# Decoder trunk, two layers, one core: six of twelve modulation sums move from TensorE to GpSimd

## The reference, cut to what matters

```python
def reference(x, c, ...):
    c_act = silu(c)
    for l in range(2):
        mod = c_act @ ada_w[l] + ada_b[l]              # 2048 -> 6144
        shift, scl, gate_res = split(mod, 3)
        h = _rms(x, norm_g[l]) * (1.0 + scl) + shift
        # layer 0: pooling mixer and block attention, layer 1: indexed attention and convolution
        y, g = branches_of(h @ w_in[l])
        x = x + gate_res * ((y * silu(g)) @ w_out[l])
    return x
```

## Time and profile before

| what | value |
|---|---|
| time, median of 3 runs | 983.06 us (979.67 to 984.81) |
| profiled execution, span | 977.3 us; its own time is not among those shown, median less span is 5.8 us |
| PE busy | 942.7 us (96%) |
| DVE busy | 822.4 us (84%) |
| ACT busy | 422.5 us (43%) |
| POOL busy | 63.5 us (6%), 76 instructions |
| granted TensorE clock, mean | 0.991 |

### The profile page before, as it was taken

One profiled execution on the slowest core, in us unless ns is written; L12 is line 12 of the kernel. 1 busy time (PEld: TensorE's weight loads), 2 busy tenths in 40 slices (PEclk: granted clock), 3 DMA queues, 4 the chain that ended last, 5 costly groups with the idle time before them and its releaser, 6 DMA issues.

```text
span 977.3 us, 18750 instructions
## 1 busy us (share of the span) xinstructions
PE 942.7 (96%) x7042; PEld 908.3 (93%) x7042; DVE 822.4 (84%) x1256; ACT 422.5 (43%) x726; POOL 63.5 (6%) x76
## 2 busy tenths in 40 slices
PE   2999999999999999999999999999999999999998
PEld 2887889999998999999999999999999989998887
DVE  5887968887999778999887999888999986879964
ACT  2220125444655444444444444444556655743331
POOL 1000000010110000132100000000011100000000
PEclk9999998999999999999999999999999999999999
DMA  9999988888876878899959555544455445587962
GB/s 366 409 399 399 379 298 319 293 329 330 325 286 233 294 260 312 322 370 377 339 176 321 193 176 189 175 151 140 164 175 193 172 163 203 199 315 288 360 227 75
DMA packets 77666, 261.26 MB, mean 267 GB/s; under 512 B 7952, under 2 KB 8592, under 8 KB 77344
## 3 DMA queue, kind: packets, MB, share of 16 engines
q1 hardware_dynamic: 72384, 240.90, 67.5%
q10 hardware_dynamic: 2880, 10.49, 2.7%
q0 software_dynamic: 2336, 8.98, 2.6%
HBM read 256.07 MB, written 4.19 MB: 266 GB/s over the span
## 4 chain that ended last, share of the span: by engine, by line
PE 72%; DVE 19%; DMA 4%; issue 2%; ACT 2%; SPq 1%; DVEq 0%; ACTq 0%
PE bank L835 13%; PE bank L836 13%; PE bank L837 13%; PE bank L856 6%; DVE wlo L1204 5%; PE bank L893 4%; PE bank L980 4%; DVE acc L1214 4%; PE bank L983 4%; PE bank L982 4%; PE bank L854 3%; DMA Y<-ada_units 3%; DVE Y L1431 2%; PE bank L927 2%; DVE acc L1234 1%
## 5 line engine op out<-in xcount | busy, mean ns | idle before, releaser
L496 ACT ACTIVATE whi<-raw 128x1024 fp32r<-128x1024 f32 x256 | 270.1, 1060 | 382.3 <-PE bank L837 217.0
L1204 DVE TENSOR_TENSOR wlo<-raw,whi 128x1024 fp32r<-128x1024 f32 x256 | 312.0, 1234 | 74.9 <-ACT whi L496 73.6
L835 PE MATMUL bank<-hhi,whi 128*128 128x256 f32 x912 | 263.8, 289 | 2.5 <-ACT T L741 0.9
L836 PE MATMUL bank<-hlo,whi 128*128 128x256 f32 x912 | 259.3, 284 | 0.0
L837 PE MATMUL bank<-hhi,wlo 128*128 128x256 f32 x912 | 259.1, 284 | 0.0
L1214 DVE SCALAR_TENSOR_TENSOR acc<-ada,cact,acc 128x1024 f32<-128x1024 f32 x144 | 187.4, 1302 | 23.9 <-DMA ada<-ada_units 12.6
L835 PEld LDWEIGHTS bank<-hhi,whi 128*128 128x128 f32 x912 | 176.2, 193 | 5.3 <-issue 3.1
L836 PEld LDWEIGHTS bank<-hlo,whi 128*128 128x128 f32 x912 | 176.2, 193 | 0.1
L837 PEld LDWEIGHTS bank<-hhi,wlo 128*128 128x128 f32 x912 | 176.1, 193 | 0.0
L980 PE MATMUL bank<-whi,hhi 128*128 128x256 f32 x512 | 146.7, 287 | 0.0
L982 PE MATMUL bank<-whi,hlo 128*128 128x256 f32 x512 | 144.9, 283 | 0.0
(11 more groups left out here) (195 smaller groups left out, 1220.2 us busy)
## 6 DMA issues: line engine op xcount, KB each, us to landing
raw<-w_slabs SPq DMA_DIRECT2D x260, 512.0 KB, 4.5
ada<-ada_units SPq DMA_DIRECT2D x160, 512.0 KB, 6.6
raw<-w_slabs ACTq DMA_DIRECT2D x20, 512.0 KB, 7.0
V<-ada_units SPq DMA_DIRECT2D x16, 512.0 KB, 9.7
Y<-ada_units SPq DMA_DIRECT2D x16, 512.0 KB, 11.3
X<-xT SPq DMA_DIRECT2D x1, 2048.0 KB, 12.6
x_dram<-X POOLq DMA_DIRECT2D x4, 512.0 KB, 8.5
outT<-X POOLq DMA_DIRECT2D x3, 512.0 KB, 4.9
```

The lines of the kernel that those rows point to most:

```text
L496: act.activation(whi[:, slot], raw[:, slot], ACT.Copy).then_inc(hi_done, 1)
L835: mm(out, whi[:, s, k, :], ahi[:, c, :], start=(c == 0), stop=False)
L836: mm(out, whi[:, s, k, :], alo[:, c, :], start=False, stop=False)
L1204: dve.tensor_tensor(wlo[:, s], source, whi[:, s].bitcast(F32), ALU.subtract)\
```

## The change

Pieces 4, 5, 6, 7, 10 and 11 are summed by POOL: `sum_piece(p)` waits for the piece's last unit, runs `partition_all_reduce` over 128 partitions x 1024 columns in place (every partition then holds the sums), and issues eight transfers, each of 128 sums from partition 0 into one column of 128 partitions of a new tile `sums`. Each raises `col_sum` by 16. `keep_piece` and `clear` wait for `col_sum` where the piece is one of these. The sums of pieces 0 to 3, 8 and 9 stay on PE.

```diff
+ON_PE, ON_POOL = (0, 1, 2, 3, 8, 9), (4, 5, 6, 7, 10, 11)
...
+            def sum_piece(p):
+                i = ON_POOL.index(p)
+                pool.wait_ge(ada_done, UNITS * (p + 1) + 4)
+                own(pool.partition_all_reduce(acc[:, p % 2, :], acc[:, p % 2, :], P, bass.bass_isa.ReduceOp.add))
+                for j in range(HC):
+                    pool.dma_start(sums[:, i, j:j + 1], acc[0:1, p % 2, j * P:(j + 1) * P]).then_inc(col_sum, 16)
+
             def clear(piece):
-                pool.wait_ge(mod_sum, piece - 1)
+                p = piece - 2
+                if p in ON_PE:
+                    pool.wait_ge(mod_sum, ON_PE.index(p) + 1)
+                else:
+                    pool.wait_ge(col_sum, 16 * HC * (ON_POOL.index(p) + 1))
                 pool.memset(acc[:, piece % 2, :], 0.0).then_inc(acc_zero, 1)
...
             pool.dma_start(PW, pool_w).then_inc(pw_in, 16)
+            sum_piece(4)
             clear(6)
             load_x(0, 0)
             load_x(0, 1)
             slopes(0, range(0, 2))
+            sum_piece(5)
             clear(7)
             slopes(0, range(2, HC))
...
+            sum_piece(6)
             clear(8)
+            sum_piece(7)
+            clear(9)
             pool.wait_ge(pt_done, HC)
             add_square(0)
             add_square(1)
-            clear(9)
...
             load_x(1, 1)
+            sum_piece(10)
+            sum_piece(11)
             for m in range(3):
                 store_x(1, m)
...
-                if w == 20:
-                    reduce_piece(4)
             for w in range(V0, G0 + 5):
-                if w == V0 + 4:
-                    reduce_piece(5)
...
-            slab(42, None, hhi, hlo, between=with_piece(6))
...
-            slab(50, None, ghi, glo, between=with_piece(7))
...
-            slab(124, None, hhi, hlo, between=with_piece(10))
...
-            slab_both(133, None, between=with_piece(11))
...
             def keep_piece(p, first=0):
-                dve.wait_ge(mod_sum, p + 1)
+                if p in ON_PE:
+                    dve.wait_ge(mod_sum, ON_PE.index(p) + 1)
+                else:
+                    dve.wait_ge(col_sum, 16 * HC * (ON_POOL.index(p) + 1))
                 keep_cols(p, first, HC).then_inc(mod_done, 1)
```

More of the change, by code:

```diff
@@ L152, in build @@
         rc = sb("rc", [P, 16])
+        sums = sb("sums", [P, len(ON_POOL), HC])
         psum = [ctx.enter_context(nc.psum_tensor(f"bank{i}", [P, 512], F32)) for i in range(8)]
@@ L175, in build @@
         mod_done = sem("mod_done")
+        col_sum = sem("col_sum")
         cexp = sem("cexp")
@@ L924, in reduce_part @@
                         pe.wait_ge(mod_done, p)
-                    if p >= 6:
-                        pe.wait_ge(o_copied, HC if p < 10 else 2 * HC)
+                    if p >= 8:
+                        pe.wait_ge(o_copied, HC)
                 ins = mm(O[:, j:j + 1], acc[:, p % 2, j * P:(j + 1) * P], ones[:, 0:1], start=True, stop=True)
@@ L934, in reduce_piece @@
                     reduce_part(p, j)
-            def with_piece(p):
-                return lambda c: c < HC and reduce_part(p, c)
             def qk_stats(w, t, q0):
@@ L1023, in attend @@
                     pe.wait_ge(z_free[b], (v0 + 1 - b) // 2 + 1 + 2 * (h // 4 + 1))
-                    pe.wait_ge(mod_done, 6 if layer == 0 else 10)
+                    pe.wait_ge(mod_done, 4 if layer == 0 else 10)
                     if a:
@@ L1118, in _ @@
                 attend(0, V0, w)
-            run(pe, 37, 42, slab_h)
-            slab(42, None, hhi, hlo, between=with_piece(6))
-            run(pe, 43, O0, slab_h)
+            run(pe, 37, O0, slab_h)
             pe.wait_ge(glo_done, KC - 2)
             slab(48, None, ghi, glo, KC)
-            slab_g(49, None)
-            slab(50, None, ghi, glo, between=with_piece(7))
-            run(pe, 51, AB1, slab_g)
+            run(pe, 49, AB1, slab_g)
             pe.wait_ge(stat_done, 2 * KC - 2)
@@ L1178, in _ @@
                     spread_token(2)
-            run(pe, 117, 124, slab_h)
-            slab(124, None, hhi, hlo, between=with_piece(10))
+            run(pe, 117, 125, slab_h)
             pe.wait_ge(glo_done, 2 * KC - 2)
             slab_both(125, None, 2 * KC)
-            run(pe, 126, 133, slab_both)
-            slab_both(133, None, between=with_piece(11))
-            run(pe, 134, N_SLABS, slab_both)
+            run(pe, 126, N_SLABS, slab_both)
         @block.vector
@@ L1237, in keep_cols @@
             def keep_cols(p, c0, c1):
-                return dve.tensor_tensor(mod[:, p * HC + c0:p * HC + c1], O[:, c0:c1],
+                source = O if p in ON_PE else sums[:, ON_POOL.index(p), :]
+                return dve.tensor_tensor(mod[:, p * HC + c0:p * HC + c1], source[:, c0:c1],
                                          par[:, C_ADAB + p * HC + c0:C_ADAB + p * HC + c1], ALU.add)
             def keep_piece(p, first=0):
-                dve.wait_ge(mod_sum, p + 1)
+                if p in ON_PE:
+                    dve.wait_ge(mod_sum, ON_PE.index(p) + 1)
+                else:
+                    dve.wait_ge(col_sum, 16 * HC * (ON_POOL.index(p) + 1))
                 keep_cols(p, first, HC).then_inc(mod_done, 1)
```

## The result

Three further timed executions and the profiled one put the change at **998.1 us** median (997.5 to 1002.5) against 983.0 (979.7 to 984.8) for the kernel before in the same session: ratio 1.018, 95% interval 1.015 to 1.021, so slower, by 1.5 to 2.1%. The profiled execution is the slowest of them, 1002.5 us with a span of 1000.7; the other three have spans of 995.8 to 996.3. Where its trace is set against that of before (span 977.3), some 4.5 us of the difference belong to this execution and not to the change, and about 4 more to the trace of before: a time lies 1.8 us above its span in every run of the change, so the median of before, 983.0, stands for a span of 981.2 and not 977.3.

A forecast was written before the change was run, and what follows sets the result against it. It took PE (busy 942.7 of 977.3 us) as the bound, with DVE where slabs lack cover. Terms -1.7 (4), +3.4 (5), -1.7 (6), -1.0 (7), +16.2 (10, 11) sum to +15.2 on 983.1: about 998 us, range 973 to 1045.

The forecast's parts named there:

- rival A: The forecast itself: u from 20 to 33, +6 to about +59 us, own range 988 to 1042; chance 0.36.
- u: T plus S, from a piece's last addition to its column sums having landed: 23 us.
- tail: Pieces 10 and 11: DVE falls behind, slab 135 on PE starts late; +16.2 us together, the largest term.
- pieces 4, 6 and 7: Gains from removing PE's sums: 1.7, 1.7 and 1.0 us, the first two covered by slack, the last partly lost.
- T: GpSimd's sum instruction over 1024 columns: 15 us, two two-input passes (11) plus 4; bounds 3.2 and 38.
- S: Eight small transfers after the sum, to the last landing: 8 us, between 6.9 and 18.7.
- R: Reload of GpSimd's code before another kind of instruction: 2.6 us, between 0.25 and 8.6.
- Piece 5: Slopes of head 2, behind the sum, a clear and a reload on GpSimd, reach DVE late: +3.4 us.
- The first output store: Stands behind sum 11 in GpSimd's queue, leaves some 30 us later, still before the last stores; nothing charged.
- Rival D: Every sum late: T from 28 to 38; at 28, +73 us and 1056 us; chance 0.14.
- Rival B: Faster: sum costs one two-input pass, 5.5 us, u 12.5, nearly every slack holds; 974 us; chance 0.34.
- C's range: Balance: u from 15.5 to 19.6, early gains paid back at the tail, within 0.5% of 983; chance 0.16.

The follow-up runs named there:

- after: Profiled execution of the change itself, all six sums on GpSimd, against the kernel before: 1002.5 us, span 1000.7; median of the change 998.1 us, ratio 1.018.
- e1_reload_end: The change plus one GpSimd iota, read by nobody, behind the last store; against the kernel before: 999.2 us, ratio 1.021.
- e_tail: Kernel before with pieces 10 and 11 alone summed on GpSimd, and an iota at the end: +3.8 us, ratio 1.004.
- e_idle6: Kernel before plus six GpSimd sums over 864 columns that nobody reads, TensorE still summing every piece, and an iota at the end: 990.7 us, ratio 1.010.
- micro: Separate kernel without the computation, timing GpSimd sums alone and beside DVE instructions, reloads and small transfers: 6.11 us for a sum of 1024 columns alone.
- e_ds4: The change with four slope buffers in place of two, and an iota at the end; against the kernel before: 1000.6 us, ratio 1.017.

## Why the prediction was right, and where it was not

The total was right, 998 forecast and 998.1 measured, and slower was the side with the most weight. That it came so near is luck: rival A stood on a u of 20 to 33, and u was 13.5 to 16.7. The tail was put 12 us too high, pieces 4, 6 and 7 were put 11 us too low, and the two errors cancelled.

- **T, 15 us: over by twice.** 6.1 to 7.0 measured. "Two two-input passes ... plus 4" had no row behind the count of passes; the lower of my rows, one pass and 5.5 us, was the nearer. Above 6.1 it is the sum's wait for an instruction of DVE. With it went **u, 23**: 13.5 to 16.7.
- **S, 8 us: right.** 4.3 to 4.5 us of issue and a landing, 6.2 to 9.8 in all. It stayed far under the 18.7 that taking turns with the weights would have cost. That bound had 128 pieces to a transfer; the software queue's packets grew from 2336 to 3872 in the pages, 32 for each of the 48.
- **R, 2.6 us: under by four times.** 10.1 to 11.4 in `after`, 8.9 at the least in `e1_reload_end`. I took it from a transfer's landing for want of a row; the 0.25 us of the earlier trace rows showed, as I noted, code that was there already. Piece 5 by my own formula with the measured values: 16.7 + 11.4 - 22.2 = +5.9 in place of +3.4; the stage grew by 4.7. But the slopes' wait is 0 to 2.3 of it.
- **Tail, +16.2: four times too much.** The stages grew by 4.6, `e_tail` measured +3.8. The formula stands; with u = 16.2 it gives 2 x 16.2 - 29.8 = +2.6.
- **Pieces 4, 6 and 7, gains of 4.4: the step that failed.** "Covered" was said of the wait, and the sums were covered: nobody waited for 4, 6 or 7. PE's gain came too, 1.8 us at piece 6. What I charged at nothing was what the sum does to DVE while it runs: one instruction held for 4.3 us. The stages cost +2.7, 0 and +4.1.
- **The start**: a wait of 12 us on POOL that I did not see. No cost could be shown.
- **The first output store** left 46 us later (909.5 to 955.2), not 30; no row of an engine waits for it.
- **Rival D** takes 3.7 us off the lateness of piece 4 (36 less 27.3 is 8.7, not 5) without saying from where. It decides nothing.

The forecast's own formula with all measured values, R in it, gives -1.7 (4) + 5.9 (5) - 1.7 (6) - 1.7 (7) + 2.6 (tail) = +3.4 us, and the runs say +15 to +20. The difference is 12 to 17 us, and stalls of DVE make most of it: `e_idle6` shows 10 to 12 us of them with nobody waiting, from sums that are a sixth shorter, and `micro` shows what is held and for how long. The rest, up to 5 us, is not shown apart. Rival B was right on T, a short sum, and would still have been wrong by 24 us; the u of 16.2 at the tail lay in C's range.

I named four tell-tale rows. DVE's bias row at piece 11 waits for a DMA, but 3.75 us and not over 10. The slopes' row waits for POOL, 2.31. PE has a hole ahead of slab 135 (3.2 us of wait). And "if GpSimd's row for the sum is short but the slopes are late, R is the cause" came out half true: `e_ds4` took that wait away and most of the stage's loss stayed.

Open: how the 4 to 8 us of piece 5 divide beyond what the intervals allow; why DVE is let go 1.7 us before the sum's row ends.

## What to carry to other kernels

When work goes to an idle engine, price not only its length and its readers but what it does to the neighbours while it runs: a stall shows as a longer instruction, not as a wait, so compare the busy time of every engine over the same instructions. A held instruction of 4 us costs 1 to 2 us in the middle of a stage with cover (sums 6 and 10), as much as the change had won there, and nearly its full length where PE runs dry on it (sum 7: 4.1 us, with 3 us of PE idle and a granted clock of 0.66 behind them). One idle copy of the new operation in the old kernel, read by nobody, tells this apart from a wait for its result in a single run.

## What the runs showed of the hardware

- GpSimd's sum over 128 partitions takes 5.6 ns a column and about 0.4 us (6.11 us for 1024, 0.43 for 8, in `micro`).
- While a sum of 1024 columns runs, a DVE instruction whose tensor operands are all in SBUF is held for 3.7 to 4.35 us; one with an operand in PSUM is not (`micro`). It is let go about 1.7 us before the end of the sum's row.
- A sum that starts while DVE is in such an instruction takes longer by about what that instruction has left: 6.1 us with none, 6.7 with 0.7 us left, 7.0 with 1.0 (`after`).
- Changing between the sum and ordinary instructions on GpSimd takes 5.9 to 7.7 us with idle queues and 8.0 to 12.5 us in these kernels, longer where the DMA share is higher, seen as "issue" idle time; a clear needs no change. An ordinary instruction at the end took the wait at the start from 12.3 to 0.5 us.
- Eight transfers of 512 bytes into single columns take 4.3 to 4.6 us to issue, and the last lands 2 to 5.5 us after that, 6.7 beside a 2 MB transfer (`micro`). Each is 32 packets.
